# Two-layer, two-block transformer on one core: the scan's off-diagonal blocks in pairs of heads on the halves of the array

## What is computed

```python
def step(state, inp):
    qc, lfc, vc = inp
    bcum = jnp.cumsum(lfc, axis=-2)
    kc = -jnp.expm1(lfc)
    o_inter = jnp.einsum('zbhcd,zbhde->zbhce', qc * jnp.exp(bcum), state)
    ...
    attn = jnp.sum(qc[..., :, None, :] * kc[..., None, :, :] * decay, axis=-1)
    o_intra = jnp.einsum('zbhts,zbhse->zbhte', attn, vc)
```

## Time and profile before

| | |
|---|---|
| median of 3 runs | 3520.4 us (3517.76 to 3525.31) |
| the profiled execution, its own time | 3518.99 us |
| its span | 3517.2 us |
| TensorE busy | 3220.4 us, 92% |
| VectorE, ScalarE, GpSimd busy | 1671.7, 1436.2, 1575.6 us |
| off-diagonal scores (line 1774) | 192 matmul records |
| values (lines 1788 and 1792) | 128 and 96 matmul records |
| mean granted clock of TensorE | 0.948 of full speed |

### The profile page before, as it was taken

How to read it: one execution, slowest core, us unless ns; L and a number is a source line. 1 busy time by engine, 2 the same in 40 slices (tenths; PEclk the granted TensorE clock), 3 DMA queues, 4 the chain that set the end, 5 groups by cost and what they waited for, 6 DMA issues and landing times. The chain is left out here.

```text
span 3517.2 us, 39165 instructions
## 1 busy us (share of the span) xinstructions
PE 3220.4 (92%) x14620; PEld 2502.2 (71%) x14620; DVE 1671.7 (48%) x2524; ACT 1436.2 (41%) x2281; POOL 1575.6 (45%) x870
## 2 busy tenths in 40 slices
PE   7978899999997899999999968899999986879999
PEld 6655688878765577887878735578887862758877
DVE  2774347731258433774246783433313766443320
ACT  4736433323384553333343444432223344352221
POOL 4623545544563354554465232344445432334444
PEclk8989999999898999999999978999999997889999
DMA  3111233333221122333322101223333200213333
GB/s 111 61 54 43 72 92 100 97 96 98 73 65 54 38 63 94 96 97 98 103 90 79 37 12 42 60 84 97 96 102 97 67 19 18 69 50 98 96 96 102
DMA packets 73740, 265.09 MB, mean 75 GB/s; under 512 B 8656, under 2 KB 9168, under 8 KB 73168
## 3 DMA queue, kind: packets, MB, share of 16 engines
q1 hardware_dynamic: 73552, 262.59, 24.1%
HBM read 260.46 MB, written 2.10 MB: 75 GB/s over the span
## 5 line engine op out<-in xcount | busy, mean ns | idle before, releaser
L359 POOL TENSOR_TENSOR low<-raw,high 128x1024 fp32r<-128x1024 f32 x482 | 1170.3, 2429 | 1299.5 <-ACT high L350 1276.7
L374 PE MATMUL bank<-slot_r,low 128*128 128x512 f32 (+2 forms) x3636 | 1435.2, 395 | 0.0
L375 PE MATMUL bank<-slot_r,high 128*128 128x512 f32 (+2 forms) x3636 | 1432.6, 394 | 0.0
L373 PE MATMUL bank<-slot_r,high 128*128 128x512 f32 (+1 forms) x3316 | 1340.5, 404 | 99.7 <-POOL low L359 22.4
L350 ACT ACTIVATE high<-raw 128x1024 fp32r<-128x1024 f32 x482 | 507.3, 1054 | 848.0 <-PE bank L375 813.9
L373 PEld LDWEIGHTS bank<-slot_r,high 128*128 128x128 f32 x3316 | 637.1, 192 | 286.8 <-issue 69.5
L374 PEld LDWEIGHTS bank<-slot_r,low 128*128 128x128 f32 (+1 forms) x3636 | 696.6, 192 | 149.0 <-issue 9.4
L375 PEld LDWEIGHTS bank<-slot_r,high 128*128 128x128 f32 (+1 forms) x3636 | 695.9, 191 | 149.7
L1568 DVE SCALAR_TENSOR_TENSOR tmp<-padded,small,tmp 128x512 f32<-128x512 f32 x176 | 210.0, 1252 | 0.0
L834 POOL TENSOR_SCALAR tmp<-tmp,stat 128x512 f32<-128x512 f32 (+3 forms) x128 | 71.6, 559 | 193.8 <-DVE stat L809 170.0
L698 PE MATMUL bank<-slots 64*128 64x256 f32 (+4 forms) x384 | 95.8, 508 | 44.5 <-PEq L320 40.7
(11 more groups left out here) (308 smaller groups left out, 3751.3 us busy)
## 6 DMA issues: line engine op xcount, KB each, us to landing
raw<-w SPq DMA_DIRECT2D x482, 512.0 KB, 3.6
slots<-x_in SPq DMA_DIRECT2D x4, 512.0 KB, 6.5
slots<-mem_in SPq DMA_DIRECT2D x2, 1024.0 KB, 4.9
out<-slots SPq DMA_DIRECT2D x8, 256.0 KB, 4.5
const<-const_in SPq DMA_DIRECT2D x1, 1073.5 KB, 10.6
padded<-p_in SPq DMA_DIRECT2D x2, 512.0 KB, 4.9
tmp<-masks_in SPq DMA_DIRECT2D x1, 512.0 KB, 11.4
small<-small SPq DMA_DIRECT2D x2, 231.5 KB, 2.7
```

What stands on the lines that cost most here:

```text
L359: pool.tensor_tensor(self.low[:, t % PARTS, :], self.raw[:, t % RING, :], self.high[:, t % PARTS, :].bitcast(F32), ALU.subtract).then_inc( ...
L373: pe.matmul(acc, lhs[0], rhs[1], start=first, stop=False)
L374: pe.matmul(acc, lhs[1], rhs[0], start=False, stop=False)
L375: return pe.matmul(acc, lhs[0], rhs[0], start=False, stop=last)
```

## The change

`off_scores(c)` and `scan_values(c)` are now called for a pair of heads, c = 0 to 3. In the scores each of the six blocks is made first for the even head (partitions 0 to 63, banks 2 and 3) and at once for the odd one (partitions 64 to 127, banks 4 and 5). In the values, for each time tile, the two heads' matmuls on PT follow each other, then the two on OFF; the even head's write to partitions 0 to 63 of the bank, the odd one's to 64 to 127. The number and form of the matmuls and copies stay as they are. OFF becomes a list of two buffers, each for a whole pair: the old one in tmp, and the four slots of K. ScalarE's copies go by pairs, four in a row, with a wait for the values of the pair before the last. Pair 1's scores stand behind the sums of the latents instead of in front of them. The three conversions of the latents on ScalarE stand together behind the last copies.

```diff
-        OFF = tmp[:, 4:8, :].rearrange("p a n -> p (a n)")
+        OFF = [tmp[:, 4:8, :].rearrange("p a n -> p (a n)"), wide(K)]
...
-                def off_scores(hd):
-                    c, r = hd // 2, slice(64 * (hd % 2), 64 * (hd % 2) + 64)
-                    if hd >= 2:
-                        pe.wait_ge(sem("off_ready"), 2 * (hd - 1))
...
-                    for o, k, q in pairs:
-                        mm = pe.matmul(o, k, q, start=True, stop=True)
+                def off_scores(c):
+
+                    if c >= 1:
+                        pe.wait_ge(sem("off_ready"), 4 * c)
...
+                    for second, at, k, q in blocks:
+                        for e in range(2):
+                            r = slice(64 * e, 64 * e + 64)
+                            mm = pe.matmul(banks[2 + 2 * e + second][:, at:at + P], k[r, :], q[r, :], start=True, stop=True)
                     mm.then_inc(sem("off_scored"), 1)
 
-                def scan_values(hd):
...
+                def scan_values(c):
...
+                    pe.wait_ge(sem("off_ready"), 4 * c + 4)
+                    if c == 2:
                         pe.wait_ge(sem("latent_root"), 2)
...
                     for j in range(NT):
...
+                        for e in range(2):
+                            h0 = 64 * e
+                            v = Vn[:, d, j, (c % 2) * P + h0:(c % 2) * P + h0 + 64]
+                            mm = pe.matmul(bank[h0:h0 + 64, j * P:j * P + P], v, PTf[:, 2 * c + e, j * P:j * P + P], start=(j == 0),
+                                           stop=(j == NT - 1), skip_group_check=True)
                         if w:
...
+                            for e in range(2):
+                                h0 = 64 * e
+                                v = Vn[:, d, j, (c % 2) * P + h0:(c % 2) * P + h0 + 64]
+                                pe.matmul(bank[h0:h0 + 64, (j + 1) * P:], v, OFF[c % 2][:, 1024 * e + at:1024 * e + at + w], start=False, stop=False,
+                                          skip_group_check=True)
                             at += w
-                    mm.then_inc(sem("pv_done"), 1)
+                    mm.then_inc(sem("pv_done"), 2)
...
                 off_scores(0)
-                off_scores(1)
...
-                scan_values(0)
-                for hd in range(1, 8):
-                    if hd + 1 < 8:
-                        off_scores(hd + 1)
-                    scan_values(hd)
+                for c in range(4):
+                    if c + 1 < 4:
+                        off_scores(c + 1)
+                    scan_values(c)
...
+                def off_copies(c):
+                    act.wait_ge(sem("off_scored"), c + 1)
+                    if c >= 2:
+                        act.wait_ge(sem("pv_done"), 2 * (c - 1))
+                    for e in range(2):
+                        for second in range(2):
+                            at = 1024 * e + 384 * second
+                            act.activation(OFF[c % 2][:, at:at + 384], banks[2 + 2 * e + second][:, 0:384], ACT.Copy).then_inc(sem("off_ready"), 1)
 
                 off_copies(0)
-                off_copies(1)
...
-                for hd in range(2, 8):
-                    off_copies(hd)
-                    if hd >= 4 and hd < 7:
-                        act.wait_ge(sem("latent_out"), hd - 3)
-                        act.activation(LATENT[hd - 4][0], S[:, (CQ, CQ + 1, CKV)[hd - 4], :], ACT.Copy).then_inc(sem("latent_high"), 1)
+                for c in range(1, 4):
+                    off_copies(c)
+                for i, slot in enumerate((CQ, CQ + 1, CKV)):
+                    act.wait_ge(sem("latent_out"), i + 1)
+                    act.activation(LATENT[i][0], S[:, slot, :], ACT.Copy).then_inc(sem("latent_high"), 1)
```

More of the change, by code:

```diff
@@ L1761, in score @@
                                     mm.then_inc(sem("a_scored"), 1)
-                def off_scores(hd):
-                    c, r = hd // 2, slice(64 * (hd % 2), 64 * (hd % 2) + 64)
-                    if hd >= 2:
-                        pe.wait_ge(sem("off_ready"), 2 * (hd - 1))
-                    b0, b1 = banks[2 + 2 * (hd % 2)], banks[3 + 2 * (hd % 2)]
-                    kt, qh = k_of(LAST), q_of(LAST)
[L1769 to L1772, removed]
-                    for o, k, q in pairs:
-                        mm = pe.matmul(o, k, q, start=True, stop=True)
+                def off_scores(c):
+                    if c >= 1:
+                        pe.wait_ge(sem("off_ready"), 4 * c)
+                    kt, qh = k_of(LAST), q_of(LAST)
+                    blocks = [(0, 0, S[:, kt + c, 0:P], S[:, qh + c, P:2 * P]), (0, P, K0[:, c, :], S[:, qh + c, 2 * P:3 * P]),
+                              (0, 2 * P, K0[:, c, :], Q3[:, c, :]), (1, 0, S[:, kt + c, P:2 * P], S[:, qh + c, 2 * P:3 * P]),
+                              (1, P, S[:, kt + c, P:2 * P], Q3[:, c, :]), (1, 2 * P, S[:, kt + c, 2 * P:3 * P], S[:, qh + c, 3 * P:])]
+                    for second, at, k, q in blocks:
+                        for e in range(2):
+                            r = slice(64 * e, 64 * e + 64)
+                            mm = pe.matmul(banks[2 + 2 * e + second][:, at:at + P], k[r, :], q[r, :], start=True, stop=True)
@@ L1775, in off_scores @@
                     mm.then_inc(sem("off_scored"), 1)
-                def scan_values(hd):
-                    c, h0, d = hd // 2, 64 * (hd % 2), hd // 4
-                    e0 = (c % 2) * P + h0
+                def scan_values(c):
+                    d = c // 2
                     bank = banks[(6, 7, 0, 1)[c]]
-                    pe.wait_ge(sem("off_ready"), 2 * hd + 2)
-                    if hd == 4:
+                    pe.wait_ge(sem("off_ready"), 4 * c + 4)
+                    if c == 2:
@@ L1783, in scan_values @@
                         pe.wait_ge(sem("latent_root"), 2)
-                    off = OFF[:, hd % 2 * 1024:]
                     at = 0
                     for j in range(NT):
-                        v = Vn[:, d, j, e0:e0 + 64]
-                        mm = pe.matmul(bank[h0:h0 + 64, j * P:j * P + P], v, PTf[:, hd, j * P:j * P + P], start=(j == 0),
-                                       stop=(j == NT - 1), skip_group_check=True)
                         w = (NT - 1 - j) * P
-                        if w:
-                            pe.matmul(bank[h0:h0 + 64, (j + 1) * P:], v, off[:, at:at + w], start=False, stop=False, skip_group_check=True)
+                        for e in range(2):
[3 more added lines that the diff above has]
+                                           stop=(j == NT - 1), skip_group_check=True)
```

## The result

The changed kernel takes 3483.2 us (median of four, 3482.64 to 3483.34) against 3519.6: a ratio of 0.9895, 95% interval 0.9883 to 0.9907, faster by 36.3 us. The profiled executions differ by 35.8 us (3519.0 and 3483.2), and that is what I account for.

A forecast was written before the change was run, and what follows sets the result against it. It took TensorE's order in the scan as the bound: 14.6 us gained per layer, 13.9 after ScalarE's queue, twice that 27.8 off 3519.0, giving 3491.2, and 3492 as median; range 3486 to 3508.

The forecast's parts named there:

- Scores in pairs: Off-diagonal scores in the scan: a pair of heads costs 1.53 us, as one head did; at most 1.81.
- Values in pairs: Values in the scan: two heads' column halves run together, 2.31 us per pair as for one head; at most 4.4.
- The copies' cover: ScalarE's four copies per pair end 1.74 us behind the values' beginning, 0.57 before TensorE wants the banks at 2.31.
- The sum of the new order: TensorE's scan in the first layer, added up: values from 1996.27, end at 2008.4 instead of 2023.0, 14.6 us gained.
- rival (b): The clock stays low through the scan and beyond: slower, about 3533 us, chance 0.03; low in the scan alone 3518, 0.03.
- What is late next: Scan's end: conversions queued on ScalarE start the fourth output copy at 2009.1 instead of 2008.4, 0.7 us per layer.
- the same 36-us stretch behind, shifted as a whole: Expected in the profile after: the stretch behind the scan comes earlier but is otherwise the same.
- (c): Rival: the gain is given back behind the scan, where something now hidden is waited for; about 3520 us, chance 0.02.
- the tail: Scan's end, where ScalarE's queue delays the last output copy: 0.7 us per layer, which if hidden lowers the time.

The follow-up runs named there:

- one_buffer: The changed kernel with one copy buffer for all pairs, so a pair's copies wait for the values of the pair before; 3501.3 us.
- values_only: The changed kernel with the scores again head by head within a pair and the values left in pairs; 3500.1 us.
- first_unpaired: The changed kernel with only pair 0's off-diagonal scores again head by head; 3496.7 us.
- first_twice: The changed kernel with pair 0's paired off-diagonal scores issued twice, the same results written again; 3490.2 us.
- before_sums_early: The kernel before, with the second head's scores moved behind the sums of the latents; 3510.5 us.
- before_far_first: The kernel before, with VectorE's scaling of K0 and Q3 moved ahead of the convolution's last five taps; 3504.0 us.
- after_swapped: The changed kernel with the pairs' outputs in banks 0, 1, 6, 7, so TensorE begins the next part before the last output copies; 3486.7 us.

## Why the prediction was right and wrong

- **Scores in pairs**, 1.53 us: 1.54 measured. Right.
- **Values in pairs**, 2.31: 2.31. Right, from the row with both heads together. The Trainium skill's rule (TensorE: Matmul & The Clock Gate, "The mechanism") that weight loads overlap running matmuls only where the row group differs would have meant about 4.4; the trace doesn't agree with it for column halves at 128, 256 and 384 columns.
- **The copies' cover**, 1.74 of 2.31: 1.75. Right, and `one_buffer` shows the price without it. The warning of the Trainium skill (TensorEngine Tiling (Array Packing), "PSUM Bottleneck"), that the copies out of PSUM may become the bottleneck once packing speeds TensorE up, agrees with that kernel (three waits of 1.8 us) and not with the changed one, whose scores and values wait for no copy.
- **The sum of the new order**, the step that failed: "If the clock rises at 1994.2 as now". I kept the time of the rise, 7 us behind the beginning, for a stretch whose load I had just changed. It rises at 3.5 us; values begin 7.45 us behind the beginning of the scan where I had 9.00. 1.6 us per layer. My rival (b) had the sign wrong: I asked only whether packing could keep the clock low, and it brings it up.
- **What is late next**, 0.7 us per layer for three conversions in ScalarE's queue: nothing measured, and the error is in the sum. I added up full durations, some 5.1 us from the beginning of the last pair's copies (2004.06) to the fourth output copy. ScalarE starts each before the one ahead has ended by its row: the three conversions take 1.69 together and not 3 x 0.63, the next row starting 1.56 behind theirs, and from the first of the last copies (2000.94) to the fourth output copy (2005.43) it is 4.49. TensorE goes on 1.34 us behind the start of the last row of values (2004.99), 1.27 before (2023.91, and the last such row at 2022.64). 0.6 us per layer.
- **"the same 36-us stretch behind, shifted as a whole"**: wrong by 1.5 us per layer, since its clock didn't shift with it. In (c) I asked only for work that the scan had hidden and not for what the end of the scan sets.
- **The chance part**: 1.6 us ahead of the first scan. With that code unchanged, the scan begins between 1984.65 and 1987.27 in the ten traces of kernels without VectorE's early scaling, and the trace of the kernel before happens to be the latest. I had nothing for it in the range. By the reasons that I gave, my lower end would even have been 3488 (3492 less 1.4 for the tail and 2.6 for the spread of the runs) and not 3486; and 3491.2 and 1.4 are 3492.6, which I put at 3492.

The excess over my 27.8 us: 2 x (1.6 + 0.6 - 0.1) in the scan (the 0.1 by which the values and scores from the first values on are longer than I summed), 2 x 1.5 behind it, 1.6 ahead of it, less 0.7: 8.1, against 8.0 measured. The size of the pairing was right; the clock, at the beginning of the scan and behind it, was what I had left standing still, and 1.6 of the 8 us are luck.

## What to carry to other kernels

Pair matmuls of 64 rows or of 64 output columns, adjacent in program order, and cost them at half, also with mixed widths where the two neighbours are equally wide; then look at who empties the banks, since here a second copy buffer was worth half of the gain. When an edit changes what TensorE does behind a wait, don't keep the instant at which the clock rises: cost the stretch at both levels and widen the range by the difference, there and in every later stretch that ends in few matmuls on the critical path. And look at the wait itself first: moving eight small VectorE instructions ahead of five long ones gave 7.5 us here and 13 on the kernel before, by a wait 3.1 us shorter per layer and a clock that then didn't fall.

## What the runs showed of the hardware that I had not expected

- With the scan's first scores on both halves of the array the granted clock was back at 1.00 after 3.4 us, with one half at a time after 6.8 (10.2 in the second layer of `values_only` and of `first_unpaired`), although TensorE was equally busy by the profile in the first 3.4 us (3.33 of 3.40 in `first_twice`, `first_unpaired` and `before_sums_early`).
- The clock's falls further on don't move exactly with the program. The same part took 58.8 or 60.2 to 60.6 us; in the two layers of `before_far_first` the step lies between a fall 17.61 us behind TensorE's going on (58.81 us) and one 17.69 behind (60.61). One case of 28, at 19.9, doesn't fit.
- Even unpaired heads overlap a little where they use different halves and nothing stands between them: 4.10 instead of 4.62 us for two heads' values.

What stays open: why the last 2 to 3 us further behind come and go (seen in `one_buffer`, `first_unpaired`, `before_sums_early`, `after_swapped`), and what makes the beginning of the first scan differ by up to 2.6 us between traces. With one trace per kernel I can't tell a difference between kernels from one between executions; those of the kernel before alone lie up to 9.6 us apart (3515.7 to 3525.3). I take the first for the same cause, a later fall of the clock, but tried no kernel on it.
